# Padding in front of tiles so that TensorE's operands start on multiples of 512 bytes

## The reference

```python
h = rms_norm(x, attn_norm)
q_lat, kv_lat, k_rope_raw, g_mla, u_lru, g_lru, m_mla, m_lru = split(h @ w_in)
y_mla = mla_branch(...)      # 16 heads, chunk-causal softmax attention, gated by silu(g_mla), @ w_o_mla
y_lru = rglru_branch(...)    # causal conv of 4 taps, two block-diagonal gates, linear scan, silu(g_lru), @ w_o_lru
merged = sigmoid(m_mla) * y_mla + sigmoid(m_lru) * y_lru
x = x + merged @ w_out
x = x + (p @ w_ple) * sigmoid(rms_norm(x, ple_norm) @ w_ple_gate)
out = rms_norm(x, final_norm)
```

## The kernel before, in words

| tiles | start, modulo 512 bytes, before | after |
|---|---|---|
| `raw`, `whi`, `wlo`, `stage`, `ident`, `ones`, `maskl`, `maskr` | 128 | 0 |
| `hhi`, `hlo`, `pthi`, `ql..`, `kv..`, `krw2`, `kr..`, `qn..`, `kn..`, `v..`, `pj..`, `qr`, `o..`, `l..`, `m..`, `x1..` | 160 | 0 |
| `xc`, `xchi`, `xclo`, `rr`, `ii`, `gg`, `sqa` | 224 | 0 |
| `graw`, `gwhi`, `gwlo` | 192 | 0 |

## Time and profile before

### The profile page before, as it was taken

How to read it: one execution, slowest core, us unless ns; L and a number is a source line. 1 busy time by engine, 2 the same in 40 slices (tenths; PEclk the granted TensorE clock), 3 DMA queues, 4 the chain that set the end, 5 groups by cost and what they waited for, 6 DMA issues and landing times.

```text
span 2126.2 us, 25597 instructions
## 1 busy us (share of the span) xinstructions
PE 2070.6 (97%) x9070; PEld 1661.5 (78%) x9070; DVE 665.4 (31%) x952; ACT 718.2 (34%) x1251; POOL 910.8 (43%) x683
## 2 busy tenths in 40 slices
PE   7999999999999999999998999999999999999997
PEld 5788888888887878778776777778888888888885
DVE  5100000000013728364676445591010151111344
ACT  6322223222223443524344444422222222233232
POOL 2444444444444544545361321144444444444442
PEclk9999999999999999999999999999999999999998
DMA  6533333333322323233352412343332343224222
GB/s 229 178 118 100 118 118 117 121 118 118 116 102 88 110 79 102 96 118 94 108 121 79 138 61 64 113 179 132 123 118 100 118 156 138 82 98 180 99 99 99
DMA packets 128684, 247.00 MB, mean 116 GB/s; under 512 B 15053, under 2 KB 40309, under 8 KB 120565
## 3 DMA queue, kind: packets, MB, share of 16 engines
q1 hardware_dynamic: 116688, 185.09, 26.6%
q10 hardware_dynamic: 11941, 61.17, 7.7%
HBM read 214.26 MB, written 29.36 MB: 115 GB/s over the span
## 4 chain that ended last, share of the span: by engine, by line
PE 51%; issue 27%; POOL 17%; DVE 3%; ACT 1%; POOLq 1%; ACTq 0%; DVEq 0%
PE ps L1214 49%; POOL wlo L351 17%; PE ps L1412 1%; DVE qrf L990 0%; DVE qrf L986 0%; POOLq L350 0%; DVE pjlo L1059 0%; PE ps L1474 0%; ACT pjhi L669 0%; DVE x L1203 0%; DVE stage L988 0%; ACTq L555 0%; POOLq L347 0%; DVE vlo L1026 0%; DVE latkv L974 0%
## 5 line engine op out<-in xcount | busy, mean ns | idle before, releaser
L351 POOL TENSOR_TENSOR wlo<-raw,whi 128x512 fp32r<-128x512 f32 x672 | 909.5, 1357 | 1189.5 <-ACT whi L367 1188.9
L367 ACT ACTIVATE whi<-raw 128x512 fp32r<-128x512 f32 x672 | 422.3, 632 | 1217.6 <-PE ps L1214 1165.9
L1214 PE MATMUL ps<-hhi,whi 128*128 128x512 f32 x1408 | 556.7, 395 | 2.9 <-POOL wlo L351 2.9
L1214 PE MATMUL ps<-hhi,wlo 128*128 128x512 f32 x1408 | 556.2, 395 | 0.0
L1214 PE MATMUL ps<-hlo,whi 128*128 128x512 f32 x1408 | 556.1, 395 | 0.0
L1214 PEld LDWEIGHTS ps<-hhi,whi 128*128 128x128 f32 x1408 | 263.9, 187 | 69.4 <-POOL wlo L351 5.1
L1214 PEld LDWEIGHTS ps<-hhi,wlo 128*128 128x128 f32 x1408 | 263.9, 187 | 64.7
L1214 PEld LDWEIGHTS ps<-hlo,whi 128*128 128x128 f32 x1408 | 263.9, 187 | 64.4
L875 DVE TENSOR_TENSOR stage<-ps,stage 128x512 f32<-128x512 f32 x16 | 11.0, 690 | 515.4 <-ACT stage L466 513.9
L1214 PE MATMUL ps<-lhi,whi 128*128 128x512 f32 x256 | 101.9, 398 | 2.5 <-DVE llo L795 2.5
L1214 PE MATMUL ps<-llo,whi 128*128 128x512 f32 x256 | 101.8, 398 | 0.0
(11 more groups left out here) (249 smaller groups left out, 2462.4 us busy)
## 6 DMA issues: line engine op xcount, KB each, us to landing
raw<-in_w_in SPq DMA_DIRECT2D x88, 1024.0 KB, 5.0
raw<-in_w_o_lru SPq DMA_DIRECT2D x16, 1024.0 KB, 5.0
raw<-in_w_o_mla SPq DMA_DIRECT2D x16, 1024.0 KB, 5.0
raw<-in_w_out SPq DMA_DIRECT2D x16, 1024.0 KB, 5.1
raw<-in_w_ple_gate SPq DMA_DIRECT2D x16, 1024.0 KB, 5.0
sig_scr<-stage ACTq DMA_DIRECT2D x8, 1024.0 KB, 7.0
raw<-in_w_kv_b SPq DMA_DIRECT2D x32, 256.0 KB, 4.2
stage<-sig_scr ACTq DMA_DIRECT2D x8, 1024.0 KB, 4.8
```

The source lines that it names most:

```text
L351: pool.tensor_tensor(wlo[:, k % RING], raw[:, k // RAWC, k % RAWC], whi[:, k % RING].bitcast(F32), ALU.subtract).then_inc(lo_ready, 1)
L367: act.activation(whi[:, c % RING], raw[:, c // RAWC % 2, c % RAWC], ACT.Copy).then_inc(hi_ready, 1)
L1214: return pe.matmul(o, l, r, start=start, stop=stop)
```

## The change

Two unused tensors and one unused tile are allocated: `line_pad` (96 numbers, 384 bytes a partition) in front of `raw`, `small_pad` (120 numbers, 480 bytes) behind the small tensors, and `upad_pad` (112 numbers, 448 bytes) behind `upad`, with `lru_pad` made shorter to match. Nothing reads or writes them. All other lines stay.

```diff
--- before.py
+++ after.py
@@ -132,6 +132,7 @@
                 return [place.enter_context(nc.sbuf_tensor(n, s, d)) for n, s, d in tensors]
 
 
+        sb("line_pad", [P, 96])
         raw = sb("raw", [P, 2, RAWC, W])
         whi = sb("whi", [P, RING, W], F32R)
         wlo = sb("wlo", [P, RING, W], F32R)
@@ -150,6 +151,7 @@
         snb = sb("snb", [P, 2, TT])
         srs = sb("srs", [P, 2, TT])
         sri = sb("sri", [P, 2, TT])
+        sb("small_pad", [P, 120])
 
 
         R1, R2 = 2 * KD * S, 2 * KD * S
@@ -158,11 +160,11 @@
             ("xraw", [P, TT, D], F32), ("sqj", [P, TT, D], F32),
             ("praw", [P, TT, PLE], F32), ("vrow", [P, 2, P], F32),
             ("pthi", [P, KP, S], F32R), ("ptlo", [P, KP, S], F32R))
-        _, upad, xc, xchi, xclo, rr, ii, gg, sqa, _, graw, gwhi, gwlo = lay(
+        _, upad, _, xc, xchi, xclo, rr, ii, gg, sqa, _, graw, gwhi, gwlo = lay(
             ("lru_r1", [P, R1], F32),
-            ("upad", [P, 4, S + 3], F32), ("xc", [P, 4, S], F32), ("xchi", [P, 4, S], F32R),
+            ("upad", [P, 4, S + 3], F32), ("upad_pad", [P, P - 16], F32), ("xc", [P, 4, S], F32), ("xchi", [P, 4, S], F32R),
             ("xclo", [P, 4, S], F32R), ("rr", [P, 4, S], F32), ("ii", [P, 4, S], F32),
-            ("gg", [P, 4, S], F32), ("sqa", [P, S], F32), ("lru_pad", [P, R2 - 4 * (S + 3) - 25 * S], F32),
+            ("gg", [P, 4, S], F32), ("sqa", [P, S], F32), ("lru_pad", [P, R2 - 4 * S - P - 25 * S], F32),
             ("graw", [P, KD, 2 * P], F32), ("gwhi", [P, 4, 2 * P], F32R), ("gwlo", [P, 4, 2 * P], F32R))
         (_, qlhi, qllo, kvhi, kvlo, cosT, sinT, latq, latkv, tsw, krz, tmp, krw, krw2, posi, _, krhi, krlo) = lay(
             ("lat_r1", [P, R1], F32),
```

## The result

The changed kernel takes 2081.73 us in the median of 4 runs (2079.4 to 2082.44), the kernel before 2130.24 us in the runs beside it. The ratio is 0.9771, 95% interval 0.9757 to 0.9785: 2.3% faster, 48.5 us. The forecast was 2078 us.

What follows compares the result with a forecast made beforehand. TensorE's matmul starts, 233.3 ns apart, were taken as the bound. Span 2126.2 - 55.5 + 0.3 (half clock) + 2.2 + 1.9 (waits) = 2075.1 us, plus 3.2 to the median: 2078 us; range 1976 to 2131.

Steps and rivals of the forecast that it cites:

- twenty intervals: Matmuls with `krw2`, both tiles at offset 160: twenty start distances in 4.53 us, 226.5 ns each, taken as the new rate.
- the term of the sum: All 8064 matmuls and the gates' 96 go from 233.3 to 226.5 ns: 55.5 us less.
- the likeliest case: Rival A, the forecast: equal offsets settle at 226.5 ns a matmul; 2078 us, range 2070 to 2105; chance 0.40.
- Its own upper end of 2105 us: Upper end of rival A's range, meant for only a third of the gain coming, as after stalls.
- the three slow streams: `features`, `tokens` and the recurrence's gates: 233.3 ns a matmul, stationary and streamed tiles differing by 32 bytes modulo 64.
- paid pair by pair: Each matmul streams one tile while the next one's weights load from another; the cost was told for each such pair.
- The new waits: Waiting that swallows part of the gain: 2.2 us in the recurrence's four rounds, 1.9 us in the attention.
- B (absolute position): Rival: operands on a 512-byte line are read without extra steps, 213 to 222 ns a matmul, 1976 to 2044 us; chance 0.27.
- C: Rival: no effect, the extra 20 ns belong to float32r at full rate; 2129 us; chance 0.24.
- its two outs: The no-effect rival's other explanations: the quicker rows came from operand order, or other engines' reads matter.
- D: Rival: tiles all on one offset make stream and weight load collide at each start, 6.8 ns more, 2185 us; chance 0.09.

Runs made afterwards that it cites:

- the kernels at 160 throughout: Changed kernel with line_pad 8 numbers instead of 96, so every tile TensorE reads starts at 160 modulo 512: 2083.14 us, ratio 0.9781 to the kernel before.
- at 0 and 256: Changed kernel with small_pad 56 numbers instead of 120: rings at 0, activation, attention and gate tiles at 256 modulo 512; 2082.13 us, ratio 0.9774.
- no offset in the table: Kernels of matmuls alone, stationary and streamed tiles at many offsets; float32r with 512 columns took 226.7 to 236.7 ns between starts.

## Why the prediction was right

**The rate.** Taken: 226.5 ns from twenty intervals. Measured: 226.7 (2.72 us for twelve), in each stage. With the real 6.67 ns the term of the sum is 54.4 us, where 55.5 stood. The long streams did settle, and within a few matmuls. The forecast had 0.40 behind it and a range wide enough for no change at all (2131 us); what the runs bear out is the likeliest case and its mechanism, not the range. (Its own upper end of 2105 us isn't what its condition gives: a third of 55.5 us leaves some 2111 us.)

**What was read into the rows.** That equal offsets are the cause is shown by the kernels at 160 throughout and at 0 and 256, and by the ring moved back by 32 bytes. Three parts of my reading were wrong and, by luck, didn't matter for this change: the three slow streams "differ by 32 bytes modulo 64" is true, but the period is 256, not 64 (128 costs 233.3 ns, 64 in one role 229); and the cost isn't paid pair by pair. Nor is it only "in proportion to the columns": that was read from the `krhi` matmuls, whose tiles start equal already (both at 160) and which took no less after the change, while in a stream at equal offsets 256, 384 and 512 columns all cost 13.3 ns more than the columns' own time. That no row showed the pair 0 and 0 was a fair reason for a wide range; as the kernel at 160 shows, it is worth what 160 and 160 are.

**The new waits.** The recurrence's wait for `wlo` was to grow from 2.4 to about 4.6 us; it is 4.7. The attention was to swallow 1.9 us and swallowed, with the queries' rope part, 4.2. This is the term that was mis-sized. I had counted waiting, which was about right (some 1.5 us), and no change of the clock, and two falls of it cost the other 2.7 us. The forecast for the span was 51.1 us less, and it fell by 45.5: 1.1 us are the rate, 2.3 the attention, 0.4 the recurrence (2.6 for 2.2), 1.4 the start (0.8 us later instead of 0.6 sooner, by the table; in the experiments it came at 51.1 to 52.1 us, whatever the offsets), and the rest crumbs. The medians differ by 48.5 us, and the 2078 us is off by 3.7.

**The rivals.** B (absolute position): no offset in the table goes below 226.7 ns, and 160 with 160 is as good as 0 with 0. Of its argument that the loss goes with what is read at the full rate, one part holds: bfloat16, with half the bytes, is 2.5 ns above the columns' time, float32r 13.3 at best. The other doesn't: the 13.3 don't grow with the columns. C: refuted by the ratio; the order of operands and other engines' reads, its two outs, are refuted by the kernels that differ in a pad alone. D: no shared offset in the table is slower than the 233.3 ns of before (the slowest is 230.0, both at 16).

**The two rules cited.** The page "TensorE: Matmul & The Clock Gate" of the Trainium skill (section "Wait — 56ns, not 53.3ns?") has 215.7 ns between starts for 512 columns at the full clock. That is what bfloat16 does here (215.8), and float32r doesn't reach it at any offset tried. The page "SBUF — State Buffer" of the Trainium skill (section "Who interferes with whom") has the stream and the weight load on independent read ports and TensorE waiting for no one. The runs don't bear out, for float32r, that the two have nothing to do with each other: the stationary tile's address alone changed the rate (streamed tile at 0, stationary at 0 and at 32 bytes: 226.7 and 233.3 ns). Whether that comes about at the ports or inside the engine isn't shown.

**What stays open.** Why a float32r stream has these steps (226.7, some 229, 231, 233.3 ns), and why two of them can be steady at one pair of offsets. The rhythm that settles depends on the addresses, on the length of the stream and on the width of the load, and at some offsets two runs of the same kind differ; I have no run that shows a mechanism. A `krhi` matmul, whose stream has no load beside it, costs more for each column though its tiles start equal before and after: after the change it takes 1136.63 - 1136.26 = 0.37 us for 512 columns and 1135.14 - 1134.94 = 0.20 us for 128, the 57 ns for 128 columns more of the earlier trace rows again, and all sixteen of 512 columns lie between 0.37 and 0.38 us in both traces. Why it pays so for its columns and a steady stream at equal offsets doesn't is open. Why the clock fell at two places of the attention is open too, and so is whether the change has to do with it: it fell at both in the kernels at 160 and at 256 as well, but at the first of them also in the kernel with activations at 64 and in the one with `wlo` off by 32 bytes, which has the old rate; and some runs of the kernel before have a mean clock as low as the ones after.

## What to carry to other kernels

Where float32r matmuls with 128 columns to load and 512 to stream run back to back at the full clock, lay the stationary and the streamed tiles so that they start equal modulo 256 bytes (and at a multiple of 32); pads of some 1.3 KB a partition in all did it here, and it was worth 2.3%. For shorter streams and narrower stationary tiles measure first: there equal offsets gained next to nothing or lost. Look for it in the distances of matmul starts, not in busy time, which stood at 97% before and after; and look at every tile of the group, since one odd one in three took back the gain of all. bfloat16 matmuls showed no such cost at the two offsets tried.

## What was new about the hardware

- 512 columns of float32r cost 226.7 ns at best and 233.3 ns at most of the offsets tried, 427 ns at the half clock, where the columns' own time is all; bfloat16 costs 215.8 ns at either offset tried.
- A difference of 4 bytes between the two tiles is the worst seen, 236.7 ns.
- For shorter streams equal offsets were not better: 384 columns took 173.3 ns at difference 0 and at 32, 256 columns 120.0 ns at 0 and 116.8 ns at 32.
